# Waiting for each transfer of the sums of the second feed-forward weights

## The chip, the cores and the metric

The kernel runs on one core of a Trainium2 chip. Its engines are TensorE (PE, matrix products; PEld is its weight load), VectorE (DVE), ScalarE (ACT), GpSimd (POOL) and SyncE (SP), each with its own instruction stream; 16 DMA engines are shared by the queues that SP, ACT and POOL fill. The metric is the device time in microseconds (us) of one execution. Lower is better.

## The reference

One decoder layer over 512 positions of width 1024, in float32:

```
x = mixer_block(x, ...)        # three mixers, gates, output projection, residual
x = cross_attention(x, mem...) # 4 heads into 256 memory tokens, residual
x = swiglu_ffn(x, g_ffn, w_ffn_in, w_ffn_out)
return rmsnorm(x, g_final)

def swiglu_ffn(x, g, w_in, w_out):
    h = rmsnorm(x, g)
    gate, up = split(h @ w_in, 2)       # hidden width 2816
    return x + (silu(gate) * up) @ w_out
```

## The kernel before

Every float32 product is made as three matmuls of operands split into a high and a low part (`mm3`, lines 1756 to 1758). Weights come in panels of 128 x 2048 floats (1 MB): SP loads a panel into `raw`, ACT writes the high part, DVE the low part (helper lines 524 and 1091), and PE multiplies. Two slots are in turn, and semaphores tell each engine when a slot is full or free.

Several of the larger products are made by a scheme with seven products in place of eight, and that needs sums of blocks of the weights. For the product with `w_ffn_out` (`fo_in`, six blocks of 128 x 512 for each of NP = 10 pairs of hidden tiles) these sums are made in the chip's main memory, without any compute engine: POOL issues transfers that copy four blocks of a pair into `fo_sums` (1024 KB), then add three blocks onto them (768 KB, `accum_op=ALU.add`), and then add two of the results onto two others (512 KB). The second of these reads and writes what the first wrote, and the third what the second wrote. So the loop of lines 484 to 493 works on three pairs at a time: in step `s` it issues the copy of pair `s`, the first addition of pair `s-1` and the second addition of pair `s-2`, and then waits for all that has been issued (`pool.wait_ge(sums_made, made[0])`, where `made[0]` counts 16 for each transfer). There are 12 steps and 30 transfers. The same is done before for other weights (`w_sums`, `together`, lines 441 to 481).

POOL carries out its program in order. Behind the loop stands `sum_squares(x2_ready, res_acc)` (lines 495 to 509): for each of the eight tiles of X, as DVE adds the residual to it (line 1450, `x2_ready`), POOL squares it (line 500) and adds it up (line 503). PE sums the result over the partitions inside the first query panel (`q_panel(0)`: wait on `res_acc`, then `sum_columns`, line 1802), for the RMS norm of the queries; later DVE, POOL and PE spread the factor.

The sums `fo_sums` are read by SP's last loop (lines 383 to 402), which waits for all of them once (line 391) before its first load.

At the point where the mixer ends, ACT's queue loads X again (line 827) and brings back the keys and values that had been stored to main memory (line 829); PE's `score(0)` waits for these.

Of the kernel before, what the change touches and what calls it, by code (L numbers as in the profile page):

```python
# [86 lines left out]
def build(nc, first_in, weights, fo_in, x_in, xt_in, memt_in, cols_in, sgu_in, wg_in, ln_g_in, ln_b_in, gf_in, out):  # L87
# [119 lines left out]
    with ExitStack() as ctx:  # L207
# [3 lines left out]
        def sem(name):  # L211
            return ctx.enter_context(nc.semaphore(name))
# [80 lines left out]
        sums_made = sem("sums_made")  # L293
# [116 lines left out]
        def _(pool):  # L410
# [23 lines left out]
            made = [0]  # L434

            def transfer(dst, src, **kw):

                made[0] += 16
                pool.dma_start(dst, src, **kw).then_inc(sums_made, 16)
# [44 lines left out]
            for step in range(NP + 2):  # L484
                if step < NP:
                    transfer(fo_sums[step], fo_in[step, :, 0:4 * S].rearrange("p (b c) -> p b c", b=4))
                if 1 <= step <= NP:
                    q = step - 1
                    transfer(fo_sums[q, :, 1:4, :], fo_in[q, :, 3 * S:6 * S].rearrange("p (b c) -> p b c", b=3), accum_op=ALU.add)
                if step >= 2:  # L490
                    q = step - 2
                    transfer(fo_sums[q, :, 0:4:2, :], fo_sums[q, :, 1:4:2, :], accum_op=ALU.add)
                pool.wait_ge(sums_made, made[0])

            def sum_squares(ready, done):

# [1835 lines left out]
```

## Time and profile before

| | us |
|---|---|
| median of 3 runs | 881.57 (881.34 to 883.61) |
| the profiled execution | 881.42 |
| its span | 879.7 |
| PE busy | 870.1 |
| DVE busy | 655.4 |
| ACT busy | 431.5 |
| POOL busy | 90.8 |

The span runs from the first to the last instruction of the profiled execution; its own time has 1.7 us around it. An engine's busy time counts its compute instructions; waits and the issue of DMAs on the SP and ACT queues are not counted.

### The profile page before, as it was taken

The numbers are of one execution on the slowest core, as the hardware profiler recorded it, in microseconds if no ns is written. First come the engines' busy times: TensorE is split into PE (matmuls) and PEld (weight loads), VectorE is DVE, ScalarE is ACT, GpSimd is POOL, SyncE is SP. The second block draws the span as 40 slices with busy tenths as digits, with TensorE's granted clock in tenths as the row PEclk, the third lists the DMA queues.
The fourth block names the chain that finished last, engine by engine and source line by source line (L and its number), as shares of the span: only waits on it lengthen the run. The fifth ranks groups of instructions, "written<-read, shape, count | busy, mean of one in ns | idle before, by whom it ended". The sixth has DMA issues, their size and how long they took to land.

```text
span 879.7 us, 13641 instructions
## 1 busy us (share of the span) xinstructions
PE 870.1 (99%) x5372; PEld 785.0 (89%) x5372; DVE 655.4 (75%) x833; ACT 431.5 (49%) x653; POOL 90.8 (10%) x104
## 2 busy tenths in 40 slices
PE   9999999999999999999999999999999999999997
PEld 7988888999999999988888888899999999988885
DVE  6695668798677687765456475998888888788977
ACT  6555334565444454532235242455554555467555
POOL 0112011011211110024100054000000000000001
PEclk9999999999999999999999999999999999999999
DMA  9968998789899993572121122223222332466622
GB/s 343 370 235 280 323 221 225 226 244 260 263 234 261 277 214 108 192 309 103 67 96 54 43 96 96 95 68 124 95 95 97 117 119 83 127 232 228 194 92 96
DMA packets 29759, 154.09 MB, mean 175 GB/s; under 512 B 3136, under 2 KB 3264, under 8 KB 17472
## 3 DMA queue, kind: packets, MB, share of 16 engines
q1 hardware_dynamic: 18592, 105.79, 33.5%
q0 software_dynamic: 8944, 35.65, 18.0%
q10 hardware_dynamic: 2176, 12.00, 3.5%
q8 instruction: 32, 0.52, 0.2%
q14 instruction: 15, 0.12, 0.0%
HBM read 147.14 MB, written 40.37 MB: 213 GB/s over the span
## 4 chain that ended last, share of the span: by engine, by line
PE 84%; DVE 7%; DMA 3%; ACT 3%; issue 2%; SPq 1%; POOLq 0%; POOL 0%; ACTq 0%; DVEq 0%
PE psum L1756 28%; PE psum L1758 27%; PE psum L1757 27%; DMA raw<-weights 3%; DVE wl L1091 1%; ACT wh L524 1%; DVE tl L1091 1%; ACT blk L524 0%; DVE fol L1091 0%; PE psum L2045 0%; DVE blk L1091 0%; DVE w7l L1091 0%; SPq L344 0%; DVE hn L1543 0%; PE psum L2172 0%
## 5 line engine op out<-in xcount | busy, mean ns | idle before, releaser
L1756 PE MATMUL psum<-th,w7h 128*128 128x256 f32 x504 | 142.7, 283 | 0.3 <-ACT snap L524 0.3
L1757 PE MATMUL psum<-tl,w7h 128*128 128x256 f32 x504 | 142.6, 283 | 0.0
L1758 PE MATMUL psum<-th,w7l 128*128 128x256 f32 x504 | 142.6, 283 | 0.0
L1091 DVE TENSOR_TENSOR wl<-raw,wh 128x2048 fp32r<-128x2048 f32 (+1 forms) x40 | 80.1, 2014 | 41.6 <-ACT wh L524 41.5
L1756 PEld LDWEIGHTS psum<-th,w7h 128*128 128x128 f32 x504 | 96.7, 192 | 0.6 <-issue 0.5
L1757 PEld LDWEIGHTS psum<-tl,w7h 128*128 128x128 f32 x504 | 96.7, 192 | 0.0
L1758 PEld LDWEIGHTS psum<-th,w7l 128*128 128x128 f32 x504 | 96.7, 192 | 0.0
L524 ACT ACTIVATE blk<-raw 128x1024 fp32r<-128x1024 f32 (+1 forms) x38 | 46.4, 1235 | 58.8 <-PE psum L1758 36.5
L524 ACT ACTIVATE wh<-raw 128x2048 fp32r<-128x2048 f32 (+1 forms) x40 | 65.5, 1652 | 14.7 <-PE psum L1758 12.1
L1756 PE MATMUL psum<-gth,blk 128*128 128x256 f32 x256 | 72.6, 283 | 0.2 <-ACT gsnap L524 0.2
L1757 PE MATMUL psum<-gtl,blk 128*128 128x256 f32 x256 | 72.4, 283 | 0.0
L524 ACT ACTIVATE snap<-psum 128x256 f32<-128x256 f32 x72 | 27.7, 384 | 84.1 <-PE psum L1758 80.8
L1756 PE MATMUL psum<-foh,hsh 128*128 128x512 f32 x156 | 61.5, 394 | 0.6 <-DVE fol L1091 0.5
L1758 PE MATMUL psum<-foh,hsl 128*128 128x512 f32 x156 | 60.8, 390 | 0.0
L1757 PE MATMUL psum<-fol,hsh 128*128 128x512 f32 x156 | 60.8, 390 | 0.0
L1756 PE MATMUL psum<-hh,blk 128*128 128x256 f32 x192 | 54.4, 283 | 0.0
L1757 PE MATMUL psum<-hl,blk 128*128 128x256 f32 x192 | 54.3, 283 | 0.0
L1756 PE MATMUL psum<-hh,wh 128*128 128x512 f32 x128 | 50.0, 391 | 0.0
L1758 PE MATMUL psum<-hh,wl 128*128 128x512 f32 x128 | 49.8, 389 | 0.0
L1757 PE MATMUL psum<-hl,wh 128*128 128x512 f32 x128 | 49.8, 389 | 0.0
L1756 PEld LDWEIGHTS psum<-gth,blk 128*128 128x128 f32 x256 | 49.1, 192 | 0.4 <-ACT gsnap L524 0.4
L1757 PEld LDWEIGHTS psum<-gtl,blk 128*128 128x128 f32 x256 | 49.1, 192 | 0.0
(296 smaller groups left out, 2355.8 us busy)
## 6 DMA issues: line engine op xcount, KB each, us to landing
raw<-weights SPq DMA_DIRECT2D x63, 1024.0 KB, 4.8
fo_sums<-fo POOLq DMA_DIRECT2D x10, 1024.0 KB, 7.1
fo_sums<-fo POOLq DMA_DIRECT2D x10, 768.0 KB, 11.1
sums<-w_sums SPq DMA_DIRECT2D x5, 1024.0 KB, 5.5
fo_sums<-fo_sums POOLq DMA_DIRECT2D x10, 512.0 KB, 13.7
raw<-fo_sums SPq DMA_DIRECT2D x10, 512.0 KB, 4.8
more<-fo_sums SPq DMA_DIRECT2D x10, 512.0 KB, 4.9
raw<-weights SPq DMA_DIRECT2D x5, 768.0 KB, 5.2
```

The lines of the kernel that those rows point to most:

```text
L524: copy = lambda o, i, **kw: nc.scalar.activation(o, i, ACT.Copy, **kw)
L1091: return V.tensor_tensor(dst, v, f32(hi), ALU.subtract)
L1756: nc.tensor.matmul(dst, lh, rh, start=start, stop=False, **kw)
L1757: nc.tensor.matmul(dst, lh, rl, start=False, stop=False, **kw)
L1758: return nc.tensor.matmul(dst, ll, rh, start=False, stop=stop, **kw)
```

## The change

After the change POOL waits after each transfer of the loop, where it waited once in each step: for the copy and for the first addition a wait is added, and the wait that stood behind the three now stands in the branch of the second addition. The transfers, their order and their bytes are the same.

```diff
             for step in range(NP + 2):
                 if step < NP:
                     transfer(fo_sums[step], fo_in[step, :, 0:4 * S].rearrange("p (b c) -> p b c", b=4))
+                    pool.wait_ge(sums_made, made[0])
                 if 1 <= step <= NP:
                     q = step - 1
                     transfer(fo_sums[q, :, 1:4, :], fo_in[q, :, 3 * S:6 * S].rearrange("p (b c) -> p b c", b=3), accum_op=ALU.add)
+                    pool.wait_ge(sums_made, made[0])
                 if step >= 2:
                     q = step - 2
                     transfer(fo_sums[q, :, 0:4:2, :], fo_sums[q, :, 1:4:2, :], accum_op=ALU.add)
-                pool.wait_ge(sums_made, made[0])
+                    pool.wait_ge(sums_made, made[0])
```

## Rows read from the trace of the kernel before

**Rows 1.** Page, busy us of each engine (share of the span) and instructions.
```profile
PE 870.1 (99%) x5372; PEld 785.0 (89%) x5372; DVE 655.4 (75%) x833; ACT 431.5 (49%) x653; POOL 90.8 (10%) x104
```
**Rows 2.** Page, shares of the chain that ended last.
```profile
PE 84%; DVE 7%; DMA 3%; ACT 3%; issue 2%; SPq 1%; POOLq 0%; POOL 0%; ACTq 0%; DVEq 0%
```
**Rows 3.** Timeline of POOL: start us, us, instruction, [idle before <-what ended it].
```profile
170.38 0.54 POOL L439 DMA_DIRECT2D fo_sums<-fo  x1 [5.67 <-DMA w_sums<-w_sums]
177.85 1.39 POOL L439 DMA_DIRECT2D fo_sums<-fo  x2 [6.92 <-DMA fo_sums<-fo]
...
326.02 0.88 POOL L439 DMA_DIRECT2D fo_sums<-fo_sums  x1 [8.47 <-DMA fo_sums<-fo_sums]
```
**Rows 4.** DMA issues (KB each, median us to landing); and reads of fo_sums, first and last start.
```profile
fo_sums<-fo POOLq DMA_DIRECT2D x10, 1024.0 KB, 7.1
fo_sums<-fo POOLq DMA_DIRECT2D x10, 768.0 KB, 11.1
fo_sums<-fo_sums POOLq DMA_DIRECT2D x10, 512.0 KB, 13.7
...
L402 SPq DMA_DIRECT2D raw<-fo_sums x10: 424/436/899, 741.5 to 823.6; - x10
```
**Rows 5.** DMA by windows from 170, 189, 315, 325 and 117 us; queues: packets, MB, share.
```profile
q1 hardware_dynamic: 144, 1.05, 42.0%
q0 software_dynamic: 142, 1.05, 35.9%
fo_sums<-fo POOLq DMA_DIRECT2D x1, 1024.0 KB, 7.2
...
fo_sums<-fo POOLq DMA_DIRECT2D x1, 1024.0 KB, 5.6
...
fo_sums<-fo POOLq DMA_DIRECT2D x1, 768.0 KB, 7.5
...
fo_sums<-fo_sums POOLq DMA_DIRECT2D x1, 512.0 KB, 7.4
...
w_sums<-weights POOLq DMA_DIRECT2D x1, 512.0 KB, 8.6
```
**Rows 6.** Timeline of POOL, the two sums of squares.
```profile
383.32 1.04 POOL L500 TENSOR_TENSOR acc<-X 128x512 f32<-128x512 f32 x1 [56.42 <-DVE X L1450]
...
421.76 1.63 POOL L503 TENSOR_TENSOR acc<-acc,sqt 128x512 f32<-128x512 f32 x1
...
515.40 1.04 POOL L500 TENSOR_TENSOR sqt<-X 128x512 f32<-128x512 f32 x1
...
518.23 1.04 POOL L500 TENSOR_TENSOR sqt<-X 128x512 f32<-128x512 f32 x1
```
**Rows 7.** Timeline of PE, the sum over the partitions.
```profile
425.04 0.95 PE L1802 MATMUL psum<-ones,acc 128*128 128x1 f32 x8
```
**Rows 8.** Waits of PE, 330 to 880 us: total us, times, longest.
```profile
PE psum L1756 <- DVE fol L1091: 0.5, 2, 0.3
```
**Rows 9.** DMA queues, 170 to 340 us.
```profile
q1 hardware_dynamic: 2448, 17.83, 29.2%
q0 software_dynamic: 5600, 23.59, 60.8%
```
**Rows 10.** DMA in 367 to 387 us, and the load issued in 370 to 375 us.
```profile
q10 hardware_dynamic: 715, 6.28, 78.3%
X<-x ACTq DMA_DIRECT2D x1, 2048.0 KB, 8.2
...
raw<-weights SPq DMA_DIRECT2D x1, 1024.0 KB, 9.4
```
**Rows 11.** Busy us of each engine, sum over 13 stretches from 170.4 to 383 us.
```profile
sum 212.60, PE 212.44 PEld 199.22 DVE 165.79 ACT 103.50 POOL 22.83; mean PE 16.34 PEld 15.32 DVE 12.75 ACT 7.96 POOL 1.76
```
**Rows 12.** Timelines of ACT and DVE, the readers of the load and of X.
```profile
388.52 1.91 ACT L524 ACTIVATE wh<-raw 128x2048 fp32r<-128x2048 f32 x1
...
382.49 0.68 DVE L1450 TENSOR_TENSOR X<-psum,X 128x512 f32<-128x512 f32 x1
```

## The prediction

> **What bounds the kernel now.** I read the page's busy rows first: TensorE (PE) is busy 870.1 of 879.7 us and GpSimd (POOL) 90.8 [rows 1]. The chain that ended last is PE for 84% of the span, and POOL has no share in it [rows 2]. So the transfers that the change spaces out, which are issued by POOL, cost nothing as long as nobody waits for them. I then followed POOL in order of time to find who could. Before the change it issues the first copy of the second feed-forward weights at 170.38 us, then groups of two or three, each released by the group before it, and the last transfer at 326.02 us [rows 3]. That one lands 7.4 us later [rows 5], so the sums are finished at 333.4 us. Only two readers are behind them: the loads on the SP queue, the first at 741.5 us [rows 4], 408 us later, and POOL's own next work, because POOL runs its program in order. This next work is the sum of squares of the residual X. Its first product starts at 383.32 us, after 56.42 us of idle, and the last addition at 421.76 us, 1.63 us long, so it ends at 423.39 us [rows 6]. PE uses it at 425.04 us (line 1802), with no wait listed there [rows 7, 8]. The slack of that hand-over is 1.65 us today, and POOL's arrival at the squares has 50 us of slack besides (383.3 less 333.4).
>
> **The change, part by part.** It adds a wait behind each copy and each first addition, and moves the existing wait into the third branch. The last step ends in that branch, so nothing is left unwaited. Twelve waits become thirty, and the same 30 transfers (10 copies of 1024 KB, 10 additions of 768 KB, 10 of 512 KB [rows 4]) go one after another. A wait instruction itself costs POOL about nothing; what counts is that each transfer pays its own way from issue to landing. POOL wakes 0.27 us after a landing (177.85 less 170.38 less 7.2) [rows 3, 5]; I use 0.25.
>
> **When it begins to cost.** If POOL comes late to the squares, X is waiting for it and it works back to back. Pairs of product and addition with the data there start 2.83 us apart (518.23 less 515.40 [rows 6]). One product of 1.04 and seven pairs make 20.9 us. With the last addition due at 425.0, POOL may arrive at 404.1 us and cost nothing; each us after that stalls PE by one us. PE waits in order there, and nothing behind takes it back: over 330 to 880 us the largest of PE's waits is 0.5 us in all [rows 8], so there is no idle time in which to catch up. The break-even is therefore (404.1 - 170.4) / 30 = 7.79 us for each transfer, or **a mean landing of 7.5 us**.
>
> **How long a transfer takes alone.** The trace has two of these kinds alone: the first copy at 7.2 us and the last 512 KB addition at 7.4 us. The ten copies, each first in its group, have a median of 7.1 us and as little as 5.6. No 768 KB addition is alone; the nearest row is the last one, at 7.5 us with only a 512 KB addition behind it [rows 4, 5]. By these a step costs 7.1 + 7.5 + 7.4 + 3 x 0.25 = 22.8 us, against 163 / 12 = 13.6 for the steps of before, and ten steps end at 398 us.
>
> Bounds. From below: the software queue keeps the engines busy 60.8% of 170 us, that is 103 us or 3.4 for each of 30 transfers [rows 9]. The copy moved in 35.9% of 7 us = 2.5 us, so the quickest landing, 5.6 us, holds 3.1 us that are not movement [rows 5]. 3.4 + 3.1 + 0.25 = 6.8 us, 203 us in all, end 373 us. From above: a 512 KB addition into the first sums, alone in its queue, took 8.6 us [rows 5]; with 8.6 for both additions a step is 7.1 + 8.6 + 8.6 + 0.75 = 25.1 us and the end is 421 us.
>
> The first copy was taken beside a load that held 42.0% of the engines in its window, while loads take 29.2% on the average of the whole stretch [rows 5, 9]. In a serial chain the engines are also freer. I take 22.0 us a step, nearer to the rows than to the floor: 390 us.
>
> One collision has to be added. At 367 us the scalar queue brings back X and four blocks of keys and values, and holds 78.3% of the engines for 20 us, 15.7 us of work [rows 10]. Before, POOL's queue was empty by then; now its last transfers are in it. The delay lies between 0 and the 15.7 us; as the engines are shared between the queues I take half, 8 us. The chain ends at **398 us**, 6 us ahead of 404.1. Term of the sum: 0.
>
> The Trainium skill ("DMA: Bandwidth & Descriptors", section on the anatomy of one DMA on the gpsimd path) gives such a transfer as about 2.0 us fixed plus its bytes at 436 GB/s: as an estimate 4.4, 3.8 and 3.2 us for the three, 12.2 us a step with the wake-ups, and an end at 292 us, earlier than today. The trace has 7.2 us where this says 4.4, so I don't use it; it would make the change safer still.
>
> **What else moves.** Loads of weights meet fewer transfers from 170 to 333 us, but PE is busy 212.44 of 212.60 us between 170.4 and 383 (the sum over stretches) [rows 11], so at most 0.2 us can be gained there. From 340 to 400 us they meet more. The load that comes in the middle of the collision (issued between 370 and 375 us) lands after 9.4 us, by 384.4 at the latest, and is read by ACT at 388.52 us [rows 10, 12]: at least 4.1 us over. X, issued just behind 367 us, lands 8.2 us later, near 375.3, and is first added at 382.49 us: about 7 us over [rows 10, 12]. The keys and values are read by score(0), which stands behind line 1802 in PE's order. One addition in flight, 3.4 us of engine time, costs these less than that. Value 0; if a cover is gone, it costs what goes beyond it.
>
> **The sum.** 881.42 us of the profiled execution (879.7 of span and 1.7 around it) + 0 = 881.4; the median of the runs is 881.57, 0.15 above it, so I forecast **881.5 us**.
>
> **Rivals.**
> 1. *POOL comes late to the squares* (slower). Place: PE's line 1802. It decides from a chain end of 404.1 us, 6 us behind my value. For it: the rows as they are give 398 us before the collision, and half the collision then makes 406 and 2 us of stall (883.7); the whole makes 414 us, 414 + 20.9 - 425.0 = 10 us of stall and 891. A middle case of 412 gives **889 us**. Against it: the loads are thinner than in those rows. A PE that idles could also come back at the lower of its two clocks. No row that I read has PE behind an idle of that length, so none prices this; I bound it by nothing and by the stall once more. The skill ("TensorE: Matmul & The Clock Gate", on the clock gate) says that an idle PE falls to 1.2 GHz; it would weigh on this rival alone. Chance 0.30.
> 2. *The queues were serial already.* In a group the landings are 7.1, 11.1 and 13.7 us apart from the issue [rows 4], that is 4 and 2.6 us after one another: they move one behind the other, and the change adds only what isn't movement. Then the lower bound holds, the end lies near 375 us, just inside the collision, and the time is **881.5 us**, the same. Chance 0.25, my own path being 0.42; the two can't be told apart by the time, only by POOL's rows.
> 3. *A load or X comes late in the collision* (slower). X would have to land over 7 us later, or the load over 4. Priced at 2 us, **883.5**, with little for it because the queues take turns. I count it inside the 0.30.
> 4. *Less contention helps* (faster). At most 0.2 us by [rows 11], unless DMA traffic also slows the engines' own reads, of which the busy PE shows no sign. **880.5 us** at the outside, chance 0.03.
>
> **How the numbers follow.** 0.3% is 2.6 us, about what a measurement of this kernel can tell. Within it lie my case and rival 2, and the stalls below 2.6 us, which I have left out of the 0.30. So faster 0.03, same 0.67, slower 0.30. The range reaches down to 880.3, a little below the lowest run, and up to the 889 of rival 1, beyond which I leave some 0.12.
>
> **What would show it.** POOL's rows of fo_sums become thirty, one at a time, 6.8 to 8 us apart, slower from 367 us on. The last is issued between 375 and 405 us. The products of the squares no longer wait for X at first but follow each other by 2.83 us, and catch up with X before its last tile. PE's line 1802 stands at 425.0. I am wrong if the last transfer lands behind 404: then line 1802 shows an idle of that excess, waiting for POOL, and everything behind it is shifted by it. I am wrong about the step if the mean landing is outside 6.5 to 7.6 us ahead of 367 us.

## The result

The changed kernel takes 886.2 us (median of 22 runs, 881.17 to 894.34) against 881.54 us (22 runs, 881.21 to 883.61). The estimated ratio is 1.0048 with an interval of 1.0033 to 1.0062, and the medians are 4.7 us apart (their quotient is 1.0053): it is slower. Five of its 22 executions took 881.2 to 881.5 us, like those of before. The forecast was no change; rival 1, POOL late at the squares, came true (it was priced at 883.7 to 891 us, with 889 as its middle case). Its profiled execution took 886.92 us, with a span of 885.2, 5.5 us over the profiled execution of before.

The changed kernel's page, engines and chain, beside [rows 1, 2]:

```profile
PE 872.6 (99%) x5372; PEld 786.7 (89%) x5372; DVE 655.7 (74%) x833; ACT 431.4 (49%) x653; POOL 93.1 (11%) x104
...
PE 44%; DMA 38%; DVE 6%; issue 5%; POOL 3%; ACT 2%; SPq 1%; POOLq 0%; ACTq 0%; DVEq 0%
DMA fo_sums<-fo 17%; PE psum L1758 14%; PE psum L1759 14%; PE psum L1760 14%; DMA w_sums<-weights 10%; DMA fo_sums<-fo_sums 6%; DMA raw<-weights 3%; DVE wl L1093 2%; POOL acc L505 1%; DMA w_sums<-w_sums 1%; POOL sqt L502 1%; ACT wh L526 1%; DVE tl L1093 1%; DVE fol L1093 0%; PE psum L2047 0%
```

The instruction counts are those of before, yet the chain that ended last now runs through the transfers of the sums for 23% of the span (17 and 6), and through POOL for 3% where it had none. PE is busy for 2.5 us more (872.6 against 870.1); the other 3.0 us of the longer span are one gap. PE's waits from 330 us on, of the changed kernel, beside [rows 8], show it (us in total, times, longest; line 1804 is 1802 of before):

```profile
PE psum L1804 <- POOL acc L505: 3.0, 1, 3.0
PE psum L1758 <- DVE fol L1093: 0.5, 2, 0.3
```

POOL's timeline of the changed kernel, beside [rows 3, 6]. The columns are start, duration, instruction and the idle time before it with what ended it:

```profile
171.11 0.54 POOL L439 DMA_DIRECT2D fo_sums<-fo  x1 [4.64 <-DMA w_sums<-w_sums]
179.67 0.52 POOL L439 DMA_DIRECT2D fo_sums<-fo  x1 [8.02 <-DMA fo_sums<-fo]
185.53 0.84 POOL L439 DMA_DIRECT2D fo_sums<-fo  x1 [5.34 <-DMA fo_sums<-fo]
...
364.32 0.89 POOL L439 DMA_DIRECT2D fo_sums<-fo_sums  x1 [8.28 <-DMA fo_sums<-fo]
370.90 0.81 POOL L439 DMA_DIRECT2D fo_sums<-fo  x1 [5.68 <-DMA fo_sums<-fo_sums]
385.76 0.88 POOL L439 DMA_DIRECT2D fo_sums<-fo_sums  x1 [14.05 <-DMA fo_sums<-fo]
399.50 0.88 POOL L439 DMA_DIRECT2D fo_sums<-fo_sums  x1 [12.86 <-DMA fo_sums<-fo_sums]
404.71 1.04 POOL L502 TENSOR_TENSOR acc<-X 128x512 f32<-128x512 f32 x1 [4.33 <-DMA fo_sums<-fo_sums]
...
411.14 1.37 POOL L502 TENSOR_TENSOR sqt<-X 128x512 f32<-128x512 f32 x1
412.58 3.25 POOL L505 TENSOR_TENSOR acc<-acc,sqt 128x512 f32<-128x512 f32 x1
415.92 1.04 POOL L502 TENSOR_TENSOR sqt<-X 128x512 f32<-128x512 f32 x1
...
424.04 2.97 POOL L502 TENSOR_TENSOR sqt<-X 128x512 f32<-128x512 f32 x1
427.09 1.26 POOL L505 TENSOR_TENSOR acc<-acc,sqt 128x512 f32<-128x512 f32 x1
```

Thirty transfers go one at a time. The 28th is issued at 370.90 us, so the first 27 took 199.8 us, 7.4 each. The last three take 33.8 us, 11.3 each. Then POOL starts the squares at 404.71 instead of 383.32, released by a transfer and not by X. It ends them at 428.35 us (427.09 + 1.26), 23.6 us later, and PE's sum starts behind an idle of 3.0 us. The DMA of the changed kernel from 367 to 387 us, beside [rows 10], shows what they meet there (queues: packets, MB, share of the engines; transfers: KB each, us to landing):

```profile
q10 hardware_dynamic: 463, 4.46, 57.0%
q0 software_dynamic: 346, 1.17, 30.4%
...
X<-x ACTq DMA_DIRECT2D x1, 2048.0 KB, 13.7
...
fo_sums<-fo POOLq DMA_DIRECT2D x1, 768.0 KB, 14.6
fo_sums<-fo_sums POOLq DMA_DIRECT2D x1, 512.0 KB, 13.5
```

The reloads of X, keys and values (q10) and the sums (q0) are on the engines together: each of the two transfers needs nearly twice its usual time. X, issued at 367.36 us, lands after 13.7 us instead of 8.2, now only some 1.6 us ahead of its reader.

After the idle PE does not return at full speed. The windows of the changed kernel from 425 us are: window, its length, busy us of PE (instructions), PEld, DVE, ACT and POOL, then the granted clock, the share of the DMA engines, GB/s:

```profile
425.00:428.40 3.40, 0.39 (x2) 0.00 (x0) 1.11 (x1) 0.00 (x0) 3.27 (x2) 1.00 0.31 72
428.40:430.00 1.60, 1.60 (x11) 1.51 (x12) 0.16 (x1) 0.00 (x0) 0.27 (x1) 1.00 1.01 430
430.00:432.00 2.00, 2.00 (x7) 1.56 (x6) 0.00 (x0) 0.00 (x0) 0.78 (x1) 0.52 0.17 66
432.00:434.00 2.00, 2.00 (x8) 1.53 (x7) 0.00 (x0) 0.00 (x0) 0.00 (x0) 0.63 0.00 0
434.00:436.00 2.00, 2.00 (x10) 1.66 (x9) 0.00 (x0) 0.00 (x0) 0.00 (x0) 1.00 0.00 0
```

The granted clock falls to half (1.2 of 2.4 GHz) about 1.6 us after PE has begun to work again, and is full once more before 434. Matmuls of 128x512 are 0.43 us apart in it instead of 0.23. The 5.5 us are 3.0 of waiting and 2.5 behind it. As an estimate from the distances of the matmuls, the lower clock makes 1.6 of the 2.5 (eight distances that are 0.20 us longer); the rest goes with the restart and was not taken apart.

### The profile page after: what moved, and what is told of

Read it like the earlier page. It is cut to its first block, busy times and chain, and to the rows that moved or that the text cites. A ratio compares the mean times of both kernels' runs of the same rounds, so it can differ in the third digit from the quotient of the medians.

```text
span 885.2 us, 13641 instructions
## 1 busy us (share of the span) xinstructions
PE 872.6 (99%) x5372; PEld 786.7 (89%) x5372; DVE 655.7 (74%) x833; ACT 431.4 (49%) x653; POOL 93.1 (11%) x104
## 4 chain that ended last, share of the span: by engine, by line
PE 44%; DMA 38%; DVE 6%; issue 5%; POOL 3%; ACT 2%; SPq 1%; POOLq 0%; ACTq 0%; DVEq 0%
DMA fo_sums<-fo 17%; PE psum L1758 14%; PE psum L1759 14%; PE psum L1760 14%; DMA w_sums<-weights 10%; DMA fo_sums<-fo_sums 6%; DMA raw<-weights 3%; DVE wl L1093 2%; POOL acc L505 1%; DMA w_sums<-w_sums 1%; POOL sqt L502 1%; ACT wh L526 1%; DVE tl L1093 1%; DVE fol L1093 0%; PE psum L2047 0%
```

## The experiments

Four questions are put: is POOL's late arrival enough to explain the loss, what does a late arrival cost and from where, why is the chain late, and does anything else in the change cost time?

### The late arrival alone, in the kernel before

No transfer is changed; POOL is held ahead of the squares by a wait on the k-th tile of X (w5 has 5, w6 has 6, w8 has 8, w4 has 4):

```diff
+            pool.wait_ge(x2_ready, 5)
             sum_squares(x2_ready, res_acc)
```

> The kernel before, with one wait more on POOL: it starts the first sum of squares only when the fifth tile of X is there (404.4 us). No transfer of the sums changes. Theory (the change costs only through POOL's late arrival at the squares, which PE waits for at its sum over the partitions): POOL works back to back from 404.5, 20.9 to 23.6 us, PE stalls by 0.4 to 3.0 us, and the time is 882 to 886.5. Rival (the transfers or the waits between them cost something of their own, and the late arrival is harmless): 881.5.

> As the run before it, with the wait on the sixth tile of X (409.6 us). Theory: the squares end at 430.6 to 433.3 us, PE stalls by 5.5 to 8.3 us, and some 2 us go to a lower granted clock behind the stall: 887 to 892. Rival: 881.5.

> As before it, with the wait on the eighth tile (420.5 us). Theory: squares end at 441.5 to 443, stall 16.5 to 18 us, 898 to 902 with the lower clock behind it. The step from the sixth tile to the eighth (10.9 us of arrival) costs 10.9 us of time if PE pays one for one. Rival: 881.5.

> The kernel before with POOL's wait on the fourth tile of X (399.2 us) ahead of the squares. By the prediction's break-even of 404.1 us nothing is lost, with 5 us over: 881.5. By the squares' length measured behind a wait (23.6 us where DVE's splits fall in them) they end at 422.8, and the eighth tile (420.5) sets the end as before: 881.4 to 882. If an arrival at 399 costs over 1 us, both are wrong.

Measured: w5 887.58 us (ratio 1.0071, 1.0055 to 1.0086), w6 892.46 (1.0123, 1.0107 to 1.0138), w8 900.84 (1.0217, 1.0201 to 1.0233), each from four executions, and w4 881.51 (0.9999, 0.9990 to 1.0008), from eleven. w5 and w6 went over the upper ends of what I expected, by 1.1 and 0.5 us. POOL's first product of the squares in the timelines of w5, w6 and w8, one fence each:

```profile
404.78 1.04 POOL L500 TENSOR_TENSOR acc<-X 128x512 f32<-128x512 f32 x1 [77.84 <-DVE X L1451]
```

```profile
409.93 1.04 POOL L500 TENSOR_TENSOR acc<-X 128x512 f32<-128x512 f32 x1 [83.17 <-DVE X L1451]
```

```profile
420.62 1.03 POOL L500 TENSOR_TENSOR acc<-X 128x512 f32<-128x512 f32 x1 [92.52 <-DVE X L1451]
```

PE's waits in the same three, in the same order:

```profile
PE psum L1803 <- POOL acc L503: 3.0, 1, 3.0
```

```profile
PE psum L1803 <- POOL acc L503: 7.9, 1, 7.9
```

```profile
PE psum L1803 <- POOL acc L503: 16.1, 1, 16.1
```

The windows of w8 in which PE resumes (granted clock third from the end):

```profile
440.00:445.00 5.00, 3.72 (x13) 3.33 (x14) 0.16 (x1) 0.00 (x0) 2.27 (x2) 0.50 0.01 3
445.00:450.00 5.00, 5.00 (x17) 3.92 (x16) 0.00 (x0) 0.00 (x0) 0.00 (x0) 0.66 0.00 0
```

POOL's timeline of w4, which has no such wait of PE:

```profile
398.80 1.04 POOL L500 TENSOR_TENSOR acc<-X 128x512 f32<-128x512 f32 x1 [71.33 <-DVE X L1451]
...
420.56 1.04 POOL L500 TENSOR_TENSOR sqt<-X 128x512 f32<-128x512 f32 x1 [0.50 <-DVE X L1451]
421.69 1.62 POOL L503 TENSOR_TENSOR acc<-acc,sqt 128x512 f32<-128x512 f32 x1
```

w5 is the decisive one. With the transfers of before, an arrival at 404.78 us gives a wait of 3.0 us and a profiled execution of 886.73 us; the changed kernel has 404.71, 3.0 and 886.92. The late arrival accounts for the whole loss of that execution. That the two times agree to 0.2 us is in part chance: the other three executions of w5 took 887.5 to 888.0 us, with the same wait on the fifth tile. The rival that the transfers cost something of their own would have left all four at 881.5. At 398.80 (w4) nothing is lost: POOL catches up and waits 0.50 us for the last tile. From w6 to w8 the medians rise by 8.4 us for 10.7 of arrival, less than one for one and short of the 10.9 that I expected; PE's wait in w8, 16.1 us, is also below my 16.5 to 18. The squares take 20.6 us in w8 and 23.3 in w6. In w8 PE and DVE stand still beside most of them, which is the likely reason.

### The reloads moved away from the chain

The changed kernel, with the keys and values brought back later:

```diff
             act.dma_start(X[:], x_in).then_inc(x_back, 16)
-            for i, part in enumerate((kh, kl, vh, vl)):
-                act.dma_start(part[:]..., kv_store[i]).then_inc(kv_back, 16)
...
             for n in range(4):
                 split_hi(WO0 + n + 1)
...
+                if n == 1:
+                    for i, part in enumerate((kh, kl, vh, vl)):
+                        act.dma_start(part[:]..., kv_store[i]).then_inc(kv_back, 16)
```

> The changed kernel, with the four reloads of keys and values issued by ACT behind the fourth tile of X (some 400 us) in place of 368 us; the reload of X stays. Theory (the last two transfers were held up by these reloads, 14 us): POOL reaches the squares at about 390 to 394 us, before the break-even of 401 to 404, no stall, 881.5. Rival (the chain is late because lone transfers are slow, wherever they stand): POOL still arrives at 400 or later, PE stalls, 884 to 887.

Measured: 881.48 us (ratio 0.9998, 0.9988 to 1.0007); one of its eleven executions took 894.8, with a granted clock of 0.993 where the other ten have 0.998 or more. It is not in the ratio, it has no profile, and its cause is open: a late chain there too is not excluded. POOL's timeline of this kernel:

```profile
369.37 0.81 POOL L439 DMA_DIRECT2D fo_sums<-fo  x1 [7.51 <-DMA fo_sums<-fo_sums]
381.85 0.88 POOL L439 DMA_DIRECT2D fo_sums<-fo_sums  x1 [11.67 <-DMA fo_sums<-fo]
387.51 0.88 POOL L439 DMA_DIRECT2D fo_sums<-fo_sums  x1 [4.79 <-DMA fo_sums<-fo_sums]
392.83 1.04 POOL L502 TENSOR_TENSOR acc<-X 128x512 f32<-128x512 f32 x1 [4.45 <-DMA fo_sums<-fo_sums]
```

The last three transfers take 23.5 us (369.37 to 392.83) instead of 33.8; only the 768 KB one, beside the reload of X that stays, is long at 12.5. The same thirty waits, with the reloads elsewhere, cost nothing in ten of eleven executions. So lone transfers are not too slow by themselves; it takes the collision to push the chain over the edge.

### The squares ahead of the last steps

The changed kernel with the loop cut at step 10 (its body made a function):

```diff
-            for step in range(NP + 2):
+            for step in range(NP):
+                sum_step(step)
...
             rsqrt(small(QR, TT), small(QV, TT), TT).then_inc(rstd_ready, 1)
+            for step in range(NP, NP + 2):
+                sum_step(step)
```

> The changed kernel, with the first sum of squares and its power placed in POOL's program behind step 9 of the sums, and the last two steps (3 of the 30 transfers, still one at a time) behind them. Theory (only POOL's order makes the late transfers cost): POOL is at the squares by about 365 us and waits for X, the last transfer lands at some 445 us, later than in any run so far, and the time is 881.5. Rival (transfers that run late cost by themselves, through loads or the clock): 884 or more.

Measured: 881.26 us (ratio 0.9999, 0.9990 to 1.0008). Its squares start as in the kernel before and its last transfer is issued 41 us later than in the changed one:

```profile
383.49 1.04 POOL L505 TENSOR_TENSOR acc<-X 128x512 f32<-128x512 f32 x1 [27.37 <-DVE X L1457]
...
440.57 0.87 POOL L439 DMA_DIRECT2D fo_sums<-fo_sums  x1 [4.70 <-DMA fo_sums<-fo_sums]
```

The transfers may end this late. They cost only because POOL's program has the squares behind them.

### Part of the change

Only the waits behind the copies (left out: those behind the first additions); and all waits, but only up to step 7:

```diff
# copy_wait, against the kernel before
                     transfer(fo_sums[step], fo_in[step, :, 0:4 * S]...)
+                    pool.wait_ge(sums_made, made[0])
# tail_group, against the changed kernel, in both places
-                    pool.wait_ge(sums_made, made[0])
+                    if step < 8:
+                        pool.wait_ge(sums_made, made[0])
```

> The kernel before with only the waits behind the copies added: the two additions of a step still go together. Lone copies land in 6.8 us and the pair in 9.7 to 11, so a step is some 17.5 us and the chain ends at 171 + 10 x 17.5 + 9 = 355 us, before the reloads. Theory (the cost is a threshold, not a price for each wait): 881.5. Rival (each added wait costs its share; 10 of 20 are here): 884.

> The changed kernel, with the waits between transfers only up to step 7, and the last four steps issued in groups as before. Step 8 starts at about 322 us (as in the changed kernel, 21.5 us a step), four grouped steps take 13.6 each, so the last one lands at 370 to 376 us, in the reloads. Theory: POOL is early enough, no stall, 881.5. Rival (a collision in itself costs time, also through X or a load): 883 or more.

Measured: copy_wait 881.62 us (ratio 1.0001, 0.9992 to 1.0010), tail_group 881.60 (0.9998, 0.9989 to 1.0008). In copy_wait the last transfer is issued at 356.97 us and lands 6.5 us later, at 363.5. I had expected the end at 355; a step takes 18.9 us there and not 17.5. It is still ahead of the reloads, and POOL then waits for X. Ten of the twenty added waits cost nothing, so there is no price for each. In tail_group the expected end of 370 to 376 us was a miss by 20. Its timeline of POOL:

```profile
331.61 1.38 POOL L439 DMA_DIRECT2D fo_sums<-fo  x2 [7.19 <-DMA fo_sums<-fo_sums]
...
360.82 0.81 POOL L439 DMA_DIRECT2D fo_sums<-fo  x1 [12.23 <-DMA fo_sums<-fo_sums]
361.34 1.19 POOL L439 DMA_DIRECT2D fo_sums<-fo_sums  x1
382.57 0.88 POOL L439 DMA_DIRECT2D fo_sums<-fo_sums  x1 [20.03 <-DMA fo_sums<-fo_sums]
396.42 1.04 POOL L504 TENSOR_TENSOR acc<-X 128x512 f32<-128x512 f32 x1 [12.97 <-DMA fo_sums<-fo_sums]
```

Step 8 began at 331.6 us and not at 322: I had taken 21.5 us for a step, but from step 2 on it takes 22.8 here and 22.7 in the changed kernel, which begins step 8 at 328.95. The last two steps, 21.8 and 13.9 us long, then ran into the reloads. The time is still that of before: a collision costs nothing while POOL comes by 396.

### The spread of the changed kernel

The changed kernel was profiled twice more.

> The changed kernel once more. Its times spread from 881.2 to 894.3 us where those of before stay within 2.4. Theory (the end of the chain moves about from one execution to the next around the break-even, and PE pays for what is over): time less 881.4 follows POOL's arrival at the squares, as in w5 and w6 (404.8 gives 5.3, 409.9 gives 11.0), and is nothing below about 401. Rival (the spread has another source): arrival and time don't go together.

> The changed kernel a third time, as the run before it: a second pair of arrival and time.

Measured: 881.70 and 891.37 us. POOL's 28th transfer and its first product in again1:

```profile
363.22 0.81 POOL L439 DMA_DIRECT2D fo_sums<-fo  x1 [5.98 <-DMA fo_sums<-fo_sums]
...
397.45 1.04 POOL L502 TENSOR_TENSOR acc<-X 128x512 f32<-128x512 f32 x1 [9.21 <-DMA fo_sums<-fo_sums]
```

and in again2, where PE's wait at its sum is 6.7 us:

```profile
375.48 0.81 POOL L439 DMA_DIRECT2D fo_sums<-fo  x1 [9.24 <-DMA fo_sums<-fo_sums]
...
408.62 1.04 POOL L502 TENSOR_TENSOR acc<-X 128x512 f32<-128x512 f32 x1 [5.11 <-DMA fo_sums<-fo_sums]
```

All profiled executions in one table, by POOL's arrival. The last column is the time less 881.42, less PE's wait:

| run | arrival | PE waits | time | rest |
|---|---|---|---|---|
| before | 383.3 | 0 | 881.42 | 0 |
| again1 | 397.5 | 0 | 881.70 | 0.3 |
| w4 | 398.8 | 0 | 881.37 | -0.1 |
| changed | 404.7 | 3.0 | 886.92 | 2.5 |
| w5 | 404.8 | 3.0 | 886.73 | 2.3 |
| again2 | 408.6 | 6.7 | 891.37 | 3.3 |
| w6 | 409.9 | 7.9 | 892.42 | 3.1 |
| w8 | 420.6 | 16.1 | 901.19 | 3.7 |

The changed and the held kernels follow the same relation of arrival and time. So the wide spread of the changed kernel's times, 13.2 us where before has 2.4, goes with the place at which its chain ends. The two repeats show where it arises: again1 comes to the 28th transfer at 363.22 us and again2 at 375.48, and the last three then take 34.2 and 33.1 us. The collision is of nearly the same length in all three profiles; the 27 ahead of it differ, at 7.14, 7.40 and 7.58 us each. Why they differ is open.

## Why the prediction was wrong

**What bounds the kernel, and who waits: right.** PE's sum at line 1802 (now 1804) was the only place, as rival 1 had it, and sq_mid shows that it is POOL's order alone that leads there.

**A step of the serial chain: right in size.** I took 22.0 us for three transfers, 7.33 each; the first 27 took 7.40. The 28th is issued 2.5 us later than my figures give (170.4 + 27 x 7.33 = 368.4, measured 370.9), 0.7 of it because the first starts at 171.11 instead of 170.38. By kind there is some luck in it: with the wake-up I had 7.35 us for a copy, 7.75 for a 768 KB addition and 7.65 for one of 512 KB, and then took 0.75 off the step. Of the first 27, from issue to issue, the copies took 6.9, the 768 KB additions 8.4 and those of 512 KB 7.0.

**The collision: the term that was mis-sized.** I gave it 8 us, half of the reloads' 15.7. The last three transfers took 33.8 us where three of 7.33 make 22.0, so it cost 11.8. Halving assumed that the two queues delay each other evenly. The addition of 768 KB took 14.9 us there instead of 8.4 and the one of 512 KB 13.7 instead of 7.0, as POOL's timeline above has it. Again1 and again2 give 12.2 and 11.1 us for the same term. With these two steps the chain ends at 398.4 (my value unrounded) + 2.5 + 3.8 = 404.7.

**The break-even: 404.1 us was too late.** I priced the squares at 20.9 us from the distance of two pairs of the later sum of squares, in which no split of a weight panel by DVE lies. Back to back behind a late start they took 23.6 (changed): two rows of them are 3.25 and 2.97 us long instead of about 1.3 and 1.0, which is 3.9 us more, while the other pairs are 2.5 to 2.8 us apart and win some of it back. So PE's need at 425 puts the edge near 401.4, and w4 (398.8, no loss) and w5 (404.8, a wait of 3.0) lie on both sides of it. My margin of 6.1 us was lost to 6.7 on the one side and 2.7 on the other, 3.3 over, against a measured wait of 3.0.

**What a stall costs: left open, and not small.** One us each, I wrote, bounded by the stall once more for the clock. It is the wait and then 2.3 to 3.7 us in every stalled run that has a profile, inside the bound that I gave but not at the nothing that the prices of rival 1 use. The Trainium skill ("TensorE: Matmul & The Clock Gate", on the clock gate) says that an idle PE falls to 1.2 GHz; the trace agrees, with granted clocks of 0.52 and 0.63 in the two windows of 2 us behind the wait, and with 0.50 in w8, inside the wait and behind it.

**The range and the chances.** Rival 1 had 0.30 and a range up to 889, and its mechanism, PE paying for what is over a limit, was right, with the limit some 3 us too late. With a chain end that was uncertain by more than its margin, two errors on the same side decided it. At a threshold with 6 us of margin behind thirty transfers, 0.2 us more for each transfer is enough. Rival 2 is refuted by the 7.1 to 7.6 us a transfer ahead of the collision in the three profiles (it wanted 6.8 and an end near 375). Rivals 3 and 4 left no trace: the largest other waits of PE are unchanged, and no run was faster than before beyond its interval.

## What to carry to other kernels

- A chain of transfers "off the critical path" has a due time: the first instruction behind it on the engine that issues it. Work out that time, divide the margin by the number of transfers, and look for what else the DMA engines are given in the stretch into which the chain is moved. The collision with a bulk reload cost 11.8 of the reload's 15.7 us of work here, three quarters and not half.
- If that margin is within the uncertainty of the estimate, the chain's tail can go behind the due work: sq_mid cost nothing in any of its ten executions. Moving the bulk reload away (kv_late) gave the time of before in ten of eleven; by its profile POOL comes 8.6 us ahead of the edge, so a margin is still wanted.

## What the runs showed of the hardware

- A PE that waited for 3.0 us ran at half clock for some 3.5 us shortly after it had resumed; after waits of 6.7 to 16.1 us the loss was 3.1 to 3.7 us, little more than after 3.0. The stall of 3.0 us cost 5.5 us, that of 16.1 us 19.8. In w6 and w8 the clock was down to 0.50 from 429 us on, while PE still waited, and stayed there for 5 to 7 us after PE resumed.
- POOL's elementwise rows lengthen beside DVE's split of a weight panel. In the changed kernel the row of 3.25 us (412.58) lies over this row of DVE, and the one of 2.97 us (424.04) over the next such split:

```profile
412.40 2.29 DVE L1093 TENSOR_TENSOR wl<-raw,wh 128x2048 fp32r<-128x2048 f32 x1 [0.79 <-ACT wh L526]
...
423.28 2.83 DVE L1093 TENSOR_TENSOR wl<-raw,wh 128x2048 fp32r<-128x2048 f32 x1 [0.47 <-ACT wh L526]
```

  In w8, where DVE stands still during PE's wait, POOL's pairs are 2.46 us apart, and the only long row (3.31 us at 423.18) comes ahead of that, beside DVE's last split. Each of these rows begins while a split runs and ends 0.9 to 1.1 us after it. A split that begins while POOL's row runs is itself longer: 2.83 us at 423.28 instead of 2.29. So each seems to wait for the other's row to end. This is read from their coincidence; no run took the split away.
